# GpSimd's subtraction in the expert stage written as two instructions of 512 columns

## What is computed

```python
q = (t @ w_pq).reshape(T, PEER_HEADS, 2, PEER_HALF)           # 8 heads
s = jnp.einsum('thpk,hpnk->thpn', q, sub_keys)
top_s, top_i = lax.top_k(s, PEER_TOPK)                        # 16 of 128, two halves
cand_s = top_s[:, :, 0, :, None] + top_s[:, :, 1, None, :]
best_s, best_pos = lax.top_k(cand_s.reshape(...), PEER_TOPK)  # 16 of 256
gate = jax.nn.softmax(best_s, axis=-1)
act = jax.nn.gelu(jnp.einsum('td,thkd->thk', t, expert_down[experts]))
out = jnp.einsum('thk,thkd->td', gate * act, expert_up[experts])
```

## Time and profile before

| | |
|---|---|
| median of 3 runs | 2987.57 us (2985.94 to 2991.8) |
| the profiled execution | 2988.53 us, span 2986.7 us |
| TensorE busy | 2900.7 us, 97% of the span |
| VectorE busy | 2406.8 us, 81% |
| ScalarE busy | 1477.7 us, 49% |
| GpSimd busy | 691.8 us, 23% |
| mean granted TensorE clock | 0.988 |

### The profile page before, as it was taken

One profiled execution on the slowest core, in us unless ns is written; L12 is line 12 of the kernel. 1 busy time (PEld: TensorE's weight loads), 2 busy tenths in 40 slices (PEclk: granted clock), 3 DMA queues, 4 the chain that ended last, 5 costly groups with the idle time before them and its releaser, 6 DMA issues. The chain is left out here.

```text
span 2986.7 us, 49273 instructions
## 1 busy us (share of the span) xinstructions
PE 2900.7 (97%) x19366; PEld 2661.5 (89%) x19366; DVE 2406.8 (81%) x4049; ACT 1477.7 (49%) x2443; POOL 691.8 (23%) x374
## 2 busy tenths in 40 slices
PE   8999999999999998999999999999899999999999
PEld 7798999879889987999999888888799999988887
DVE  6878997697899765998997677776599999656665
ACT  4453334445333444446665455555444666545554
POOL 0100000010000011796664000001289666300000
PEclk9999999999999998999999999999899999999999
DMA  6445555544555552454445777873255444555554
GB/s 231 181 147 201 199 211 191 186 155 156 191 199 211 185 195 100 163 185 148 142 142 200 241 264 257 296 251 132 107 170 178 140 142 142 177 183 191 195 193 162
DMA packets 125104, 547.98 MB, mean 183 GB/s; under 512 B 13731, under 2 KB 16972, under 8 KB 100300
## 3 DMA queue, kind: packets, MB, share of 16 engines
q1 hardware_dynamic: 124716, 544.30, 52.6%
q10 hardware_dynamic: 160, 0.54, 0.0%
HBM read 540.05 MB, written 6.30 MB: 183 GB/s over the span
## 5 line engine op out<-in xcount | busy, mean ns | idle before, releaser
L2032 POOL TENSOR_TENSOR q_lo<-q_raw,q_hi 128x1024 fp32r<-128x1024 f32 x250 | 625.5, 2508 | 260.7 <-ACT q_hi L2146 260.0
L2051 PE MATMUL k_psN<-k_hhi,q_hi 128*128 128x256 f32 x2304 | 666.7, 289 | 0.6 <-ACT e_hv L2210 0.2
L2051 PE MATMUL k_psN<-k_hhi,q_lo 128*128 128x256 f32 x2304 | 652.9, 283 | 0.0
L2051 PE MATMUL k_psN<-k_hlo,q_hi 128*128 128x256 f32 x2304 | 652.7, 283 | 0.0
L2146 ACT ACTIVATE q_hi<-q_raw 128x1024 fp32r<-128x1024 f32 x538 | 565.5, 1051 | 6.9 <-DMA q_raw<-up 3.8
L2349 DVE TENSOR_TENSOR q_lo<-q_raw,q_hi 128x1024 fp32r<-128x1024 f32 x288 | 352.8, 1225 | 129.4 <-ACT q_hi L2146 128.8
L2051 PEld LDWEIGHTS k_psN<-k_hhi,q_hi 128*128 128x128 f32 x2304 | 443.0, 192 | 2.8 <-DVE k_hlo L2375 2.4
L2051 PEld LDWEIGHTS k_psN<-k_hlo,q_hi 128*128 128x128 f32 x2304 | 443.3, 192 | 0.0
L2051 PEld LDWEIGHTS k_psN<-k_hhi,q_lo 128*128 128x128 f32 x2304 | 442.4, 192 | 0.0
L760 DVE TENSOR_TENSOR k_wlo<-k_raw,k_whi 128x2048 fp32r<-128x2048 f32 x158 | 360.7, 2285 | 71.3 <-ACT k_whi L580 70.4
L580 ACT ACTIVATE k_whi<-k_raw 128x2048 fp32r<-128x2048 f32 x158 | 301.8, 1913 | 217.5 <-PE f_psA L432 102.6
(11 more groups left out here) (357 smaller groups left out, 5464.7 us busy)
## 6 DMA issues: line engine op xcount, KB each, us to landing
k_raw<-ws SPq DMA_DIRECT2D x180, 1024.0 KB, 4.8
q_raw<-down SPq DMA_DIRECT2D x288, 512.0 KB, 3.4
q_raw<-up SPq DMA_DIRECT2D x256, 512.0 KB, 3.5
k_x<-ada SPq DMA_DIRECT2D x48, 512.0 KB, 3.7
e_ada<-ada SPq DMA_DIRECT2D x48, 512.0 KB, 5.0
out<-k_x SPq DMA_DIRECT2D x3, 1024.0 KB, 3.9
k_x<-out SPq DMA_DIRECT2D x3, 1024.0 KB, 6.9
k_x<-x SPq DMA_DIRECT2D x2, 1024.0 KB, 5.9
```

Source lines behind the costliest of these rows:

```text
L2032: nc.gpsimd.tensor_tensor(lo[:, i % RING, :], raw[:, i % RING, :], hi[:, i % RING, :].bitcast(F32), ALU.subtract).then_inc(S["lo_pool"], 1)
L2051: last = nc.tensor.matmul(psD(n), w, h, start=kt == 0 and i == 0, stop=kt == KT - 1 and i == 2)
```

## The change

The subtraction of one unit is written as two GpSimd instructions, for columns 0 to 511 and for columns 512 to 1023. Only the second raises `lo_pool`, so TensorE and SP still wait for the whole unit. The wait for `hi_ready` stands once, ahead of the first. Nothing else is touched.

```diff
@@ -2029,8 +2029,9 @@
             def _(pool):
                 for i in range(RING, BY_POOL):
                     pool.wait_ge(Q["hi_ready"], i + 1)
-                    nc.gpsimd.tensor_tensor(lo[:, i % RING, :], raw[:, i % RING, :], hi[:, i % RING, :].bitcast(F32),
-                                            ALU.subtract).then_inc(S["lo_pool"], 1)
+                    for c in (slice(0, D // 2), slice(D // 2, D)):
+                        ins = nc.gpsimd.tensor_tensor(lo[:, i % RING, c], raw[:, i % RING, c], hi[:, i % RING, c].bitcast(F32), ALU.subtract)
+                    ins.then_inc(S["lo_pool"], 1)
                 if more:
                     norm_tail(nc, pool, env, (1, 3, 2, 4))
```

## The result

| | |
|---|---|
| kernel before, this comparison | 2989.34 us, median of 11 runs (2985.94 to 2994.31) |
| changed kernel | 2995.07 us, median of 11 runs (2992.74 to 2997.25) |
| ratio | 1.0017, 95% interval 1.0009 to 1.0025 |
| profiled execution of the changed kernel | 2997.25 us, span 2995.2 us |

The ratio is +5.1 us (0.0017 x 2989.34), from 2.7 to 7.5 us. That lies inside the bound of 0.2%, near its edge, and 2995.07 us lies inside the range, but above the 2987 to 2994 us of the likeliest case. The kernel before, too, took more here than in the runs that the forecast started from (2989.34 us for 2987.57).

A forecast was written before the change was run, and what follows sets the result against it. TensorE, busy 97% of the span, was read as the bound; +4.4 us (selection) + 0.2 - 1.8 us (gated start) = +2.8 us, so 2987.6 + 2.8 = 2990.4 us, counted as no change. The range is 2986 to 3000 us.

The forecast's parts named there:

- likeliest case: Whole kernel: the forecast of no change within 0.2%, chance 0.70, which alone spans 2987 to 2994 us.
- Price of the split: GpSimd's subtraction in every unit: two halves cost 0.18 us more than one whole instruction, bounds 0 and 0.35 us.
- Second part, units 17 to 58: Selection part: VectorE's pair of instructions per head makes TensorE stand, 2.2 us per layer, 4.4 us for both.
- same unit: Selection part: VectorE's pair delays both halves of one unit, 2.0 us against a 1.57 us margin; TensorE stands 0.43 us.
- neighbours: Selection part: VectorE's pair delays two adjacent units, 1.66 us against a 1.57 us margin; TensorE stands 0.09 us.
- small VectorE instructions: Selection part: smaller VectorE instructions meet more boundaries between GpSimd instructions, adding 0.1 us per head.
- Start of the gated part: Second layer: `hot2` ready earlier, TensorE gains 1.8 us, less 0.2 us for a late subtraction; first layer gains nothing.
- Low clock mark: First gated group after TensorE's wait: the lower clock level, worth 1.76 us, stays in both kernels.
- Gated part: 128 gated units cost nothing: VectorE is six microseconds ahead and GpSimd has over a microsecond to spare per unit.
- GpSimd becomes the bound: Selection part: GpSimd's load fills the stretch, some 2998 us, up to 3005; chance 0.26 together with a third delay.
- Shorter holds make it faster: Gated start: 2986 us if the second half's beginning is hidden, 2977 us if wait and low clock vanish; clearly faster 0.04.
- the halves change who comes first: Selection part: a third delay of up to 1.0 us per head, 2998 us; chance 0.26 together with GpSimd as bound.

The follow-up runs named there:

- quarters: Four GpSimd instructions of 256 columns for units 3 to 58, whole ones from unit 59 on, against the kernel before: 3009.16 us, ratio 1.0077.
- GpSimd narrow: Kernel before with ScalarE's one-hot rows early and GpSimd subtracting only columns 0 to 255 in units 64 to 127: 2989.97 us against 2991.93.

## Why the prediction held, and where it did not

*Price of the split.* 0.18 us per unit was taken; it is 0.14 (2.54 for 2.40 us). A half was put at 1.31 us and takes 1.29. The straight line through the 1-column and the 1024-column row was good to 2% for a half; the fixed part is 0.19 us where the 1-column row gave 0.22. The Trainium skill's figure (GPSIMD Engine Reference, section 3.1) gave an estimate of 0.3 us per unit. The measured 0.14 is half of it, and the measurement decides.

*Second part, units 17 to 58.* +4.4 us was predicted and 1.51 + 2.87 = 4.4 us measured, but the layers differ where both had 2.2. Predicted stalls of 0.43 (same unit) and 0.09 (neighbours) are seen as 0.40 + 0.10 and 0.04 + 0.09 us, the second number at the unit behind. With the measured 0.14 in place of 0.18 the prediction's own subtraction gives 0.39 and 0.01, near the first numbers. In the first layer two of six heads are of the costly kind, at units 34 and 47. The second layer is dearer because of the late DMA of unit 33, which the sum priced at nothing and the range named. In all five profiles with halves and both VectorE instructions in the selection part unit 33 is 1.15 to 1.16 us late. The issue comes late with `lo` of unit 30, as the chain above shows, and on top of that the transfer is slow (4.67 to 5.18 us in the five). A slow transfer alone costs nothing: with halves only from unit 59 on that of unit 33 takes 4.99 us in the second layer, and unit 33 begins on time. Why it is slow stays open. That the total agrees is therefore partly luck: 0.1 us per head for small VectorE instructions was too much, and the DMA was too little.

The removal of one VectorE instruction shows that the pair is what turns the price into a stall. The Trainium skill (SBUF — State Buffer, section "Who interferes with whom") says that a VectorE instruction with two SBUF inputs and a GpSimd instruction block each other for a whole instruction. The rows of unit 46 agree that one waits for the other: GpSimd lost 1.0 us to each of the two VectorE instructions, which take 1.22 us, and the second of them lost 1.0 us to GpSimd's first half. By the same section a reduction never contends; the row of L2316, 1.22 us beside GpSimd's second half, agrees.

*Start of the gated part.* This is the step that failed. It took 1.8 us off for the second layer, because in the profiled execution TensorE waited for `hot2` and not for ScalarE. The mechanism was read rightly: with halves `hot2` takes 1.80 us in place of 2.85 and is ready earlier, and with a late copy of unit 60 the start went from 10.55 to 8.96 us, the 1.6 us of the sum (1.8 less 0.2). But that copy is late in 3 of 28 starts. In the second execution of the kernel before it is not, `hot2` comes before ScalarE's row with whole subtractions too (8.67 us), and there is nothing to gain. A slow transfer in a single execution was taken for a property of the kernel. The changed kernel's three profiles all have 8.66 or 8.67 us, in both layers. Without the two terms the sum would be 4.4 us, where five comparisons of kernels with halves in the selection part give ratios of 1.0013 to 1.0019, 3.9 to 5.7 us.

*Low clock mark.* That it stays in both kernels was wrong as a rule: the first group takes 5.3 us or 3.84 us in the same kernel, as the table shows. At this place it takes no side between the kernels.

*Gated part.* It was free, as predicted: 237.30 us with and without halves. The reason given, "both covers are thick", holds only for this start. With ScalarE's row early VectorE was the bound, 120.00 of 120 us, and halves then saved 2.1 us per layer (245.4 for 247.5). So the six microseconds of lead hold only with the pattern of one collision per group; another pattern costs VectorE 0.3 us more in each.

*The rivals.* "GpSimd becomes the bound" did not happen with halves and did with quarters. "Shorter holds make it faster" is wrong: its way to 2977 us, an earlier ScalarE row, made the kernel 13 to 18 us slower. Of "the halves change who comes first", no third delay of 1.0 us per head is seen; a layer loses 1.5 to 2.9 us, not 6.

What stays open: why the transfers of unit 33 and, in three starts, of unit 59 take about 5 us, whether the 1.5 us between the layers belong to the change, and what sets the pattern in which VectorE and GpSimd meet in the gated part. That the absent lead at the start chooses it was only argued.

## What to carry to other kernels

Before splitting an instruction on an engine that shares something with another, put its fixed cost (here 0.14 us in 2.4) against the smallest margin in the stretch where it is loaded most, not against its share of the span: 23% busy overall was 92% where it mattered. Shorter holds help the other engine only if that engine is waited for; look at two executions of the unchanged kernel before a wait at a stage's border goes into a sum, and ask which late transfer or copy began it. And do not count an engine's lead as a cover before seeing what keeps it: a change that only removed a wait of 1 us cost 10 us per layer behind it.

## What the runs showed of the hardware

GpSimd's `tensor_tensor` with two float32 inputs takes 0.741, 1.29 and 2.40 us for 256, 512 and 1024 columns: 2.15 ns a column and 0.19 us for each instruction, of which about 0.04 us overlap with the one before.

In the gated part, where neither VectorE's own work (83 of 120 us with GpSimd nearly out of the way) nor GpSimd's (70 to 76 us) fills the time, the two together can: with whole subtractions VectorE is busy or held up for 113.5 us in one pattern and for all 120 in the other, 30 and 37 us more than with GpSimd narrow. The second pattern makes TensorE wait, 10.2 us in 237.3.

After a short idle time (1.06 us) TensorE's granted clock differs between executions of one program at the same place (1.00 or 0.83 as the mean of 226 to 236 us). With such places two executions of the changed kernel differ by 4.3 us before they reach the changed part, as much as the whole change costs.
